# Expert rows of a decoder layer: gathered as quarters and turned in 32x32 blocks on VectorE instead of TensorE transposes

## The chip, the cores and the metric

The kernel is one program on one core of a Trainium2 chip. The core has a matrix engine (TensorE, "PE" in the profile, with its weight loads as "PEld"), VectorE ("DVE"), ScalarE ("ACT"), GpSimd ("POOL"), a queue engine ("SP") and 16 DMA engines that all queues share. The metric is the device time of one execution in microseconds (us); lower is better.

## The reference, cut to what matters

The program computes one layer of a hybrid decoder: a projection, differential attention, an S5 state-space branch, an output projection, and then a mixture of experts in which each of 2048 tokens goes to 2 of 32 experts. The change touches the last part alone:

```
order = jnp.argsort(flat_e)                       # assignments sorted by expert
rows = jnp.zeros((n_rows, 1024)).at[dest].set(h[stok])   # every expert padded to blocks of 128 rows
def expert_block(args):
    xb, e = args                                  # 128 rows of 1024 values, one expert
    hid = jax.nn.silu(xb @ w_gate[e]) * (xb @ w_up[e])   # w_gate, w_up: 1024 x 512
    return hid @ w_down[e]                        # w_down: 512 x 1024
out = segment_sum(expert_out * gate, stok)        # back to the tokens
```

Everything is fp32. A matmul is done as three matmuls in the faster fp32r format: each operand is split into a high part (rounded) and a low part (the rest), and hi x hi, hi x lo and lo x hi are summed.

## The kernel before, in words

The stages before the experts write the normalised tokens to a table in HBM, `h2`, of 1024 values a row. A routing stage (`route`) makes `ids`, a 128 x 64 tile in which column b holds the token of each of the 128 rows of block b, and `meta`, which holds for each block the ordinal of its expert. With the inputs timed here there are 49 blocks over 32 experts. `place(b)` is the ordinal of block b's expert; where it differs from the block before, the weights change. This text calls such a block a change of expert, and neighbouring blocks that each change the expert a run.

`experts` is written as one loop per engine. The engines meet in semaphores alone, and each engine carries out its instructions strictly in its written order. Iteration j of the loops handles the first two products of block j+1 and the last product of block j.

- TensorE, per iteration: `product(G, 0)` (24 matmuls of 512 columns with w_gate), `hidden_T(j)` (4 transposes of the hidden values), `product(U, 1)` (24 matmuls with w_up), `rows_T(0)` and `rows_T(1)` (8 transposes of 128x128 that turn the gathered rows `x` of the block after next into PSUM banks XT), `down(j)` (24 matmuls with w_down). A transpose of rows is needed since a matmul contracts over the partitions.
- ScalarE: `hidden_hi`, silu, `split_hi(0)` twice (the high part of w_gate, 128x2048 each, only on a change of expert), `rows_hi` twice (high part of the turned rows), `split_hi(1)` (w_up) around `out_half` (scaled output rows, waits for `down`), then `split_hi(2)` (w_down, an iteration after the change).
- VectorE: `hidden_lo`, `split_lo(0)` twice (low part of w_gate), `hidden` (silu times U, waits for U), `rows_lo` twice (low part of the rows, from PSUM), `split_lo(1)` twice, `split_lo(2)` twice.
- GpSimd: waits until the transposes have read `x`, then gathers the rows of the block after (`gather`: an index column is copied, then one indirect DMA of 128 rows of 4 KB); `add_rows` (waits for both `out_half`, then an indirect DMA adds 128 rows to `x1` in HBM), `gather_gate` (128 single values), and on a change of expert the two 1 MB loads of the next w_down, each after the `split_lo(2)` that frees its half.
- SP: the loads of the next w_gate and w_up, each half after the `split_lo` that frees it.

All buffers named here exist once: one `x`, one raw, one high and one low copy of each weight.

## Time and profile before

| | |
|---|---|
| Time, median of 3 runs | 2225.64 us (2224.3 to 2226.03) |
| Time of the profiled execution | 2227.88 us |
| Its span, first to last instruction | 2226.2 us |
| Expert stage within the span | about 1254.5 to 2154 us |
| Mean granted TensorE clock | 0.949 |
| TensorE busy | 2001.2 us, 90% |
| VectorE, ScalarE, GpSimd busy | 1416.8, 1073.5, 529.1 us |

The profiled execution took 2227.88 us, of which 1.68 us lie outside the span. The page's busy shares are averages over unlike stages, so the expert stage is read by itself.

### The profile page before, as it was taken

What the parts mean: (1) busy time and instruction counts of PE and PEld (TensorE: products, weight loads), DVE (VectorE), ACT (ScalarE), POOL (GpSimd) and SP (SyncE); (2) the same over time, 40 slices, a digit from 0 to 9 for tenths busy, and PEclk for the clock granted to TensorE, in tenths of its full rate; (3) what the DMA queues carried; (4) which work ended last, traced back from release to release, by engine and by line L of the source; (5) the groups of instructions that cost most, each with busy time, mean ns of one, the idle gap of its engine ahead of it and who ended that gap; (6) DMA issues with size and microseconds to landing.
All of it is one profiled execution on the core that took longest, in us unless ns stands there. A gap on an engine that the chain in (4) does not pass through costs nothing. (4 is left out here: it accounts for less than half of the span.)

```text
span 2226.2 us, 32053 instructions
## 1 busy us (share of the span) xinstructions
PE 2001.2 (90%) x10153; PEld 1677.8 (75%) x10154; DVE 1416.8 (64%) x2368; ACT 1073.5 (48%) x1591; POOL 529.1 (24%) x637
## 2 busy tenths in 40 slices
PE   6999999886798989869997599999999999999970
PEld 5888888785587878768886488888888888888860
DVE  4675687466697977946555766575668756445444
ACT  4332211234377777862322365565567655445443
POOL 2000111242000000000000244454445645334440
PEclk9999999998799999989998699999999999999995
DMA  8665986731464143024443597797879978576638
GB/s 251 221 223 203 304 299 228 244 150 29 130 154 109 48 101 77 1 79 138 142 153 151 179 363 252 267 337 270 289 255 389 343 270 314 178 248 223 230 81 315
DMA packets 170121, 458.37 MB, mean 206 GB/s; under 512 B 19872, under 2 KB 69104, under 8 KB 144432
## 3 DMA queue, kind: packets, MB, share of 16 engines
q1 hardware_dynamic: 122896, 285.30, 37.2%
q0 software_dynamic: 31008, 138.37, 20.2%
q10 hardware_dynamic: 16128, 33.56, 4.3%
q8 instruction: 50, 0.82, 0.1%
q14 instruction: 39, 0.32, 0.1%
HBM read 342.08 MB, written 115.10 MB: 205 GB/s over the span
## 5 line engine op out<-in xcount | busy, mean ns | idle before, releaser
L2208 DVE TENSOR_TENSOR w_down_lo<-w_down_raw,w_down_hi 128x2048 fp32r<-128x2048 f32 x64 | 144.1, 2288 | 122.9 <-ACT w_down_hi L2145 122.9
L1480 PE MATMUL c_bank<-v_head,map_T 128*128 128x128 f32 x1088 | 150.8, 282 | 24.1 <-ACT map_T L1390 21.3
L1480 PEld LDWEIGHTS c_bank<-v_head,map_T 128*128 128x128 f32 x1088 | 138.1, 194 | 39.3 <-ACT map_T L1390 32.0
L2208 DVE TENSOR_TENSOR w_gate_lo<-w_gate_raw,w_gate_hi 128x2048 fp32r<-128x2048 f32 x63 | 141.6, 2288 | 40.3 <-ACT w_gate_hi L2145 33.9
L2292 PE MATMUL m_bank<-w_down_hi,hidden_T_hi 128*128 128x512 f32 x392 | 160.4, 409 | 6.8 <-DVE w_down_lo L2208 6.8
L2271 PE MATMUL m_bank<-w_gate_hi,rows_T_hi 128*128 128x512 f32 x392 | 156.2, 399 | 6.4 <-DVE rows_T_lo L2213 3.9
L2271 PE MATMUL m_bank<-w_up_hi,rows_T_hi 128*128 128x512 f32 x392 | 158.8, 405 | 0.0
L2208 DVE TENSOR_TENSOR w_up_lo<-w_up_raw,w_up_hi 128x2048 fp32r<-128x2048 f32 x64 | 146.2, 2286 | 15.7 <-ACT w_up_hi L2145 15.7
L2272 PE MATMUL m_bank<-w_gate_lo,rows_T_hi 128*128 128x512 f32 x392 | 156.0, 398 | 0.0
L2273 PE MATMUL m_bank<-w_gate_hi,rows_T_lo 128*128 128x512 f32 x392 | 156.0, 398 | 0.0
L2293 PE MATMUL m_bank<-w_down_lo,hidden_T_hi 128*128 128x512 f32 x392 | 155.3, 396 | 0.0
L2273 PE MATMUL m_bank<-w_up_hi,rows_T_lo 128*128 128x512 f32 x392 | 154.8, 395 | 0.0
L2272 PE MATMUL m_bank<-w_up_lo,rows_T_hi 128*128 128x512 f32 x392 | 154.5, 394 | 0.0
L1450 PE MATMUL c_bank<-k_parts,q_parts 128*128 128x512 f32 (+3 forms) x320 | 132.2, 418 | 10.0 <-DMA k_parts<-kT_d 5.2
L1330 DVE CUSTOM_DVE_ANT_0 scores<-c_bank,alibi 128x512 f32<-128x512 f32 (+3 forms) x160 | 97.3, 608 | 46.2 <-PE c_bank L1451 40.3
L2160 ACT ACTIVATE rows_out<-m_bank,slot_gate 128x512 f32<-128x512 f32 x98 | 67.4, 688 | 106.0 <-PE m_bank L2297 106.0
L2145 ACT ACTIVATE w_up_hi<-w_up_raw 128x2048 fp32r<-128x2048 f32 x62 | 118.5, 1914 | 0.0
L1451 PE MATMUL c_bank<-k_parts,q_parts 128*128 128x512 f32 (+3 forms) x320 | 118.4, 376 | 0.0
L2145 ACT ACTIVATE w_down_hi<-w_down_raw 128x2048 fp32r<-128x2048 f32 x62 | 115.4, 1905 | 6.2 <-DMA w_down_raw<-in_w_down_dram 6.2
L2149 ACT ACTIVATE rows_T_hi<-m_bank 128x512 fp32r<-128x512 f32 x100 | 54.5, 596 | 129.7 <-PE m_bank L2264 129.6
L2145 ACT ACTIVATE w_gate_hi<-w_gate_raw 128x2048 fp32r<-128x2048 f32 x62 | 115.3, 1916 | 0.0
L2110 POOL DMA_INDIRECT x_d<-rows_out,to_idx x49 | 109.0, 2224 | 9.9 <-issue 9.9
(422 smaller groups left out, 5226.9 us busy)
## 6 DMA issues: line engine op xcount, KB each, us to landing
w_gate_raw<-in_w_gate_dram SPq DMA_DIRECT2D x64, 1024.0 KB, 7.0
w_down_raw<-in_w_down_dram POOLq DMA_DIRECT2D x64, 1024.0 KB
w_up_raw<-in_w_up_dram SPq DMA_DIRECT2D x64, 1024.0 KB, 8.1
hT_d<-hT_parts SPq DMA_DIRECT2D x32, 512.0 KB, 5.1
hT_parts<-hT_d SPq DMA_DIRECT2D x32, 512.0 KB, 9.2
k_parts<-kT_d SPq DMA_DIRECT2D x64, 256.0 KB, 8.2
u_tok<-in_x_dram SPq DMA_DIRECT2D x16, 512.0 KB, 5.3
qT_d<-qk_out ACTq DMA_DIRECT2D x32, 256.0 KB, 3.6
```

The source lines that it names most:

```text
L1330: dve.tensor_tensor_reduce(of(u, m, c * BANK, c * BANK + w), bank[2 * (n % 2) + m][:, 0:w], ramp[:, x0:x0 + w], SLOPES[h], -BIG, ALU.add, ...
L1450: pe.matmul(out, qt, k_of(4 * h + c, 0)[:, m, 0:w].bitcast(F32R), start=True, stop=False)
L1451: pe.matmul(out, qt, k_of(4 * h + c, 1)[:, m, 0:w].bitcast(F32R), start=False, stop=True).then_inc(qk_done, 1)
L1480: last = pe.matmul(out_of(u), aT[:, n % 2, b * P:(b + 1) * P], v[h % 2][:, kt], start=kt == 0, stop=kt == u % NT)
L2110: pool.indirect_dma_start(d["x1"], bass.IndirectOffsetOnAxis(ap=to_idx[:], axis=0), out[:], None, compute_op=ALU.add).then_inc(out_st, 16)
L2145: act.activation(whi[w][:, halves[i]], raw[w][:, halves[i]], ACT.Copy).then_inc(hi_done[w], 1)
L2208: dve.tensor_tensor(wlo[w][:, halves[i]], raw[w][:, halves[i]], whi[w][:, halves[i]], ALU.subtract).then_inc(lo_done[w], 1)
L2271: pe.matmul(to[:], xh[:, k], whi[w][:, c], start=k == 0, stop=False)
L2272: pe.matmul(to[:], xh[:, k], wlo[w][:, c], start=False, stop=False)
L2273: last = pe.matmul(to[:], xl[:, k], whi[w][:, c], start=False, stop=k == KT - 1)
L2292: pe.matmul(DN[h][:], hh[:, k], whi[2][:, part(k)], start=k == 0, stop=False)
L2293: pe.matmul(DN[h][:], hh[:, k], wlo[2][:, part(k)], start=False, stop=False)
```

## The change

From the third block on, a block's rows are no longer gathered as whole rows. `h2` is seen as a table of 4 x 2176 quarter rows of 256 values, and four indirect DMAs of 128 quarters (1 KB each) fill `x`: partition 32f + i gets, in its r-th quarter, the quarter f of row 32r + i. A 128x1024 tile that lies so needs only to be transposed inside 32x32 blocks, and VectorE does that in two instructions, `turn(0)` and `turn(1)`, 512 elements a partition each, from SBUF (stride of 8 elements) to a new SBUF tile `rows_T`. The 8 TensorE transposes leave the loop. `rows_hi` and `rows_lo` read `rows_T` in SBUF and no longer XT in PSUM. The indices of the quarters are made once, at the stage's start, in `part_rows` on VectorE, with 4 small matmuls on TensorE behind the first `product(G, 0)` and before the first `product(U, 1)`.

```diff
+    def gather_parts(self, pool, ones, part_ids, d, b):
+        pool.tensor_copy(self.part_idx[:], part_ids[:, bass.ds(b * PARTS, PARTS)]).then_inc(self.idx_set, 1)
+        pool.wait_ge(self.idx_set, b + 1)
+        pool.tensor_tensor(self.hold[:], ones[:, 0:1], ones[:, 1:2], ALU.add)
+        for r in range(PARTS):
+            pool.indirect_dma_start(self.x[:, r * PART:(r + 1) * PART], None, d["h2"].rearrange("r (f c) -> (r f) c", f=PARTS),
+                                    bass.IndirectOffsetOnAxis(ap=self.part_idx[:, r:r + 1], axis=0)).then_inc(self.x_in, 16)
...
 GpSimd, before the loop
-                for b in range(2):
-                    pool.wait_ge(xT_psum, 2 * b + 2)
-                    gather(b + 1)
+                pool.wait_ge(xT_psum, 2)
+                store.gather(pool, ones, ids, d, 1)
+                pool.wait_ge(part_set, 1)
+                pool.wait_ge(xT_psum, 4)
+                store.gather_parts(pool, ones, part_ids, d, 2)
 GpSimd, in the loop
-                    pool.wait_ge(xT_psum, 2 * j + 6)
-                    gather(j + 3)
+                    pool.wait_ge(turned, 2 * j + 2)
+                    store.gather_parts(pool, ones, part_ids, d, j + 3)
 ScalarE, in the loop
+                def rows_hi(h, want):
+                    act.wait_ge(turned, want)
+                    act.activation(xh[:, 4 * h:4 * h + 4], xT[:, 4 * h:4 * h + 4], ACT.Copy).then_inc(xh_done, 1)
...
-                    rows_hi(0, 2 * j + 5)
-                    rows_hi(1, 2 * j + 6)
+                    act.wait_ge(u_done, j + 2)
+                    rows_hi(0, 2 * j + 1)
+                    rows_hi(1, 2 * j + 2)
                     with where_below(nc, act, now, order):
-                        act.wait_ge(u_done, j + 2)
                         split_hi(1, order, 0)
 VectorE
+                def rows_lo(h, want):
+                    dve.wait_ge(xh_done, want)
+                    dve.tensor_tensor(xl[:, 4 * h:4 * h + 4], xT[:, 4 * h:4 * h + 4], xh[:, 4 * h:4 * h + 4],
+                                      ALU.subtract).then_inc(xl_done, 1)
+
+                def turn(h):
+                    dve.transpose(xT[:, 4 * h:4 * h + 4].rearrange("p k (r i) -> p r k i", r=PARTS),
+                                  x[:].rearrange("p (r j k) -> p r k j", r=PARTS, k=KT)[:, :, 4 * h:4 * h + 4]).then_inc(turned, 1)
+
+                def part_rows():
+                    dve.tensor_copy(pick[:], ident[:].rearrange("p (r o i) -> p r o i", r=PARTS, o=1).to_broadcast([P, PARTS, PARTS, QUAD])).then_inc(pick_set, 1)
...
+                    dve.wait_ge(part_psum, 1)
+                    dve.tensor_scalar(part_ids[:].rearrange("p (b r) -> p b r", r=PARTS), PI[:, 0:PARTS * NBLK].rearrange("p (r b) -> p b r", r=PARTS),
+                                      float(PARTS), quad[:, 0:1], ALU.mult, ALU.add).then_inc(part_set, 1)
...
                 split_lo(1, 0, 1)
+                part_rows()
                 split_lo(2, 0, 0)
 in the loop, after split_lo(0)
+                    dve.wait_ge(x_in, 64 * j + 96)
+                    dve.wait_ge(xl_done, 2 * j + 4)
+                    turn(0)
+                    turn(1)
                     hidden(j + 1)
 TensorE, after the first product(G, 0)
+                pe.wait_ge(pick_set, 2)
+                for r in range(PARTS):
+                    last = pe.matmul(PI[:, r * NBLK:(r + 1) * NBLK], pick[:, r].rearrange("p f i -> p (f i)"), ids_f[:], start=True, stop=True)
+                last.then_inc(part_psum, 1)
 TensorE, in the loop
-                    pe.wait_ge(x_in, 16 * j + 48)
-                    rows_T(0)
-                    rows_T(1)
                     down(j, before)
```

## Rows read from the trace of the kernel before

**Rows 1.** The page, part 1: busy time of each engine.
```profile
PE 2001.2 (90%) x10153; PEld 1677.8 (75%) x10154; DVE 1416.8 (64%) x2368; ACT 1073.5 (48%) x1591; POOL 529.1 (24%) x637
```

**Rows 2.** Windows: length, busy of PE, PEld, DVE, ACT, POOL, clock, DMA share, GB/s.
```profile
1254.50:2154.00 899.50, 889.17 (x4100) 728.39 (x4100) 551.08 (x387) 510.55 (x481) 428.00 (x498) 0.99 0.78 273
...
1701.00:1719.30 18.30, 18.30 (x86) 14.98 (x86) 15.57 (x10) 13.98 (x12) 10.57 (x12) 1.00 1.02 384
```

**Rows 3.** Groups of the loop, 1300 to 2190 us.
```profile
L2213 DVE TENSOR_TENSOR rows_T_lo<-m_bank,rows_T_hi 128x512 fp32r<-128x512 f32 x94 | 60.3, 683 | 6.9 <-ACT rows_T_hi L2149 6.9
...
L2264 PE MATMUL m_bank<-ident,rows_in 128*128 128x128 f32 x376 | 49.3, 274 | 0.0
...
L2045 POOL DMA_INDIRECT rows_in<-h_d,idx x46 | 46.2, 1005 | 11.3 <-issue 10.5
```

**Rows 4.** Timeline of PE over one iteration and the start of the next.
```profile
1610.52 0.63 PE L2281 MATMUL m_bank<-ident,hidden 128*128 128x128 f32 x4
...
1616.58 1.05 PE L2264 MATMUL m_bank<-ident,rows_in 128*128 128x128 f32 x8
1617.38 0.48 PE L2292 MATMUL m_bank<-w_down_hi,hidden_T_hi 128*128 128x512 f32 x1
1617.70 0.39 PE L2293 MATMUL m_bank<-w_down_lo,hidden_T_hi 128*128 128x512 f32 x1
...
1623.07 0.40 PE L2271 MATMUL m_bank<-w_gate_hi,rows_T_hi 128*128 128x512 f32 x1
...
1628.67 0.63 PE L2281 MATMUL m_bank<-ident,hidden 128*128 128x128 f32 x4
```

**Rows 5.** Timeline of DVE: a w_down split, then an iteration with a change of expert.
```profile
1335.34 4.49 DVE L2208 TENSOR_TENSOR w_down_lo<-w_down_raw,w_down_hi 128x2048 fp32r<-128x2048 f32 x2 [6.65 <-ACT w_down_hi L2145]
...
1630.90 0.69 DVE L2223 TENSOR_TENSOR hidden_T_lo<-m_bank,hidden_T_hi 128x512 fp32r<-128x512 f32 x1 [0.61 <-issue]
1632.26 4.50 DVE L2208 TENSOR_TENSOR w_gate_lo<-w_gate_raw,w_gate_hi 128x2048 fp32r<-128x2048 f32 x2 [0.68 <-ACT w_gate_hi L2145]
1636.67 0.68 DVE L2219 TENSOR_TENSOR hidden<-silu,m_bank 128x512 f32<-128x512 f32 x1
1637.27 1.28 DVE L2213 TENSOR_TENSOR rows_T_lo<-m_bank,rows_T_hi 128x512 fp32r<-128x512 f32 x2
```

**Rows 6.** Timeline of POOL: beside the w_down split above, and in a run.
```profile
1335.47 2.20 POOL L2099 COPY gate_idx<-slot_gate_ids 128x1 int32 x1
1337.76 2.13 POOL L2101 TENSOR_TENSOR hold<-ones 128x1 f32<-128x1 f32 x1
...
1685.21 1.03 POOL L2102 DMA_INDIRECT slot_gate<-gates_d,gate_idx  x1
...
1742.23 1.16 POOL L2080 DMA_DIRECT2D w_down_raw<-in_w_down_dram  x2
...
1757.30 3.05 POOL L2102 DMA_INDIRECT slot_gate<-gates_d,gate_idx  x1
```

**Rows 7.** Timeline of ACT: the second w_down half of the load at 1742.23.
```profile
1755.21 1.91 ACT L2145 ACTIVATE w_down_hi<-w_down_raw 128x2048 fp32r<-128x2048 f32 x1 [2.38 <-DMA w_down_raw<-in_w_down_dram]
```

**Rows 8.** Timelines of DVE and PE at the start of the expert stage.
```profile
1262.37 4.48 DVE L2208 TENSOR_TENSOR w_down_lo<-w_down_raw,w_down_hi 128x2048 fp32r<-128x2048 f32 x2
1271.47 4.50 DVE L2208 TENSOR_TENSOR w_gate_lo<-w_gate_raw,w_gate_hi 128x2048 fp32r<-128x2048 f32 x2 [4.62 <-ACT w_gate_hi L2145]
...
1230.58 1.01 PE L1913 MATMUL r_bank<-ident,block_facts 128*1 128x128 f32 x4 [4.17 <-DVE block_facts L1989]
...
1268.84 0.40 PE L2271 MATMUL m_bank<-w_up_hi,rows_T_hi 128*128 128x512 f32 x1
...
1278.07 0.47 PE L2271 MATMUL m_bank<-w_gate_hi,rows_T_hi 128*128 128x512 f32 x1 [2.57 <-issue]
```

**Rows 9.** PE after a long idle stretch, then windows beside it (columns as in rows 2).
```profile
711.64 1.22 PE L1480 MATMUL c_bank<-v_head,map_T 128*128 128x128 f32 x4 [3.40 <-ACT map_T L1390]
...
712.00:718.00 6.00, 6.00 (x26) 5.28 (x26) 5.36 (x10) 4.20 (x13) 0.00 (x0) 0.58 0.01 3
```

More of the change, by code:

```diff
@@ L43 @@
 NBLK = 64
+PARTS = 4
+PART = D // PARTS
+QUAD = P // PARTS
 MIN_BLK = 2 * SEQ // P
@@ L2049, in source, with experts @@
         return a[("w_gate", "w_up", "w_down")[w]][0, e].rearrange("o (p k) n -> p (o k n)", k=k)[:, self.halves[i]]
-def experts(nc, ident, ones, ids, gate_ids, meta, store, a, d):
+def experts(nc, ident, ones, const, ids, gate_ids, meta, store, a, d):
     with ExitStack() as ctx:
@@ L2056, in experts @@
         sem = ctx.enter_context(phase_semaphores(nc))
-        bank = [ctx.enter_context(nc.psum_tensor(f"m_bank{i}", [P, BANK], F32)) for i in range(7)]
-        G, U, XT, HT, DN = bank[0], bank[1], bank[2:4], bank[4], bank[5:7]
+        bank = [ctx.enter_context(nc.psum_tensor(f"m_bank{i}", [P, BANK], F32)) for i in range(8)]
+        G, U, XT, HT, DN, PI = bank[0], bank[1], bank[2:4], bank[4], bank[5:7], bank[7]
         FT = FF // P
@@ L2071, in experts @@
         g_done, u_done, d_done, silu_done, hid_done = (sem(n) for n in ("g_done", "u_done", "d_done", "silu_done", "hid_done"))
-        xT_psum, xh_done, xl_done, hT_psum = (sem(n) for n in ("rT_psum", "rT_hi_done", "rT_lo_done", "hidT_psum"))
+        xT_psum, turned, xh_done, xl_done, hT_psum = (sem(n) for n in ("rT_psum", "rows_turned", "rT_hi_done", "rT_lo_done", "hidT_psum"))
+        pick_set, part_psum, part_set = (sem(n) for n in ("row_of_quad_set", "part_ids_psum", "part_ids_set"))
         with nc.Block() as block:
@@ L2094, in _ @@
             def _(pool):
-                gather = lambda b: store.gather(pool, ones, ids, d, b)
                 def gather_gate(b, count):
@@ L2145, in split_hi, with first_rows_hi @@
                     act.activation(whi[w][:, halves[i]], raw[w][:, halves[i]], ACT.Copy).then_inc(hi_done[w], 1)
-                def rows_hi(h, want):
+                def first_rows_hi(h, want):
                     act.wait_ge(xT_psum, want)
                     act.activation(xh[:, 4 * h:4 * h + 4], XT[h][:].rearrange("p (k t) -> p k t", k=4), ACT.Copy).then_inc(xh_done, 1)
+                def rows_hi(h, want):
+                    act.wait_ge(turned, want)
+                    act.activation(xh[:, 4 * h:4 * h + 4], xT[:, 4 * h:4 * h + 4], ACT.Copy).then_inc(xh_done, 1)
                 def hidden_hi(want):
@@ L2162, in _ @@
                 act.preload_act_table(ACT.Silu)
-                rows_hi(0, 1)
-                rows_hi(1, 2)
+                first_rows_hi(0, 1)
+                first_rows_hi(1, 2)
                 first, second = place(act, 0), place(act, 1)
@@ L2170, in _ @@
                     split_hi(0, second, 1)
-                rows_hi(0, 3)
-                rows_hi(1, 4)
+                first_rows_hi(0, 3)
+                first_rows_hi(1, 4)
                 with where_below(nc, act, first, second):
@@ L2209, in split_lo, with first_rows_lo @@
                                       ALU.subtract).then_inc(lo_done[w], 1)
-                def rows_lo(h, want):
+                def first_rows_lo(h, want):
                     dve.wait_ge(xh_done, want)
@@ L2226, in _ @@
                 split_lo(1, 0, 0)
-                rows_lo(0, 1)
-                rows_lo(1, 2)
+                first_rows_lo(0, 1)
+                first_rows_lo(1, 2)
                 split_lo(1, 0, 1)
+                part_rows()
                 split_lo(2, 0, 0)
@@ L2236, in _ @@
                 hidden(0)
-                rows_lo(0, 3)
-                rows_lo(1, 4)
+                first_rows_lo(0, 3)
+                first_rows_lo(1, 4)
                 with where_below(nc, dve, first, second):
@@ L2440, in hybrid_layer @@
             route(nc, ident, ones, logits, const, ids, gate_ids, meta, store, a, d)
-            experts(nc, ident, ones, ids, gate_ids, meta, store, a, d)
+            experts(nc, ident, ones, const, ids, gate_ids, meta, store, a, d)
         finish(nc, a, d, out)
```

12 lines of the change are left out of this document (11 added, 1 removed).

## The prediction

> **What bounds the kernel now.** I read the page's busy times first: TensorE is busy for 2001.2 of 2226.2 us [rows 1]. Then the windows, since the change touches one stage: from 1254.5 to 2154 us TensorE is busy for 889.2 of 899.5 us at a granted clock of 0.99 (the 2.4 GHz level), DVE for 551, POOL for 428 [rows 2]. So TensorE sets this stage and what leaves its queue is worth its whole length, until another queue is late. Which one could be, I read from the timelines, each time counted from the start H of the four transposes of the hidden values. TensorE: H is 1610.52, the next H 1628.67: a period of 18.15 us, without a gap. The next product with w_gate starts at 1623.07, H + 12.55 [rows 4]. DVE in an iteration with a change of expert (H = 1628.67): the w_gate split starts at H + 3.59, `hidden` at H + 8.00, and `rows_lo` ends at 1638.55, H + 9.88 [rows 5]. The rows are ready 2.67 us ahead of the product that reads them. This slack is what the two turns are put into.
>
> In the DVE timeline 30 of the 48 iterations hold a w_gate split, and one more stands ahead of the loop. By iteration they are ahead, 0, 1; 3; 5; 7 to 10; 12; 14, 15; 17; 19 to 25; 27; 29 to 31; and every second one from 34 to 46, so there are two runs of three, one of four and one of seven. In the long run the DMA engines are at 1.02 of their time [rows 2], and a half of w_down whose load was issued at 1742.23 is first read at 1755.21, after ScalarE waited 2.38 us for it [rows 6, 7]. That is 13 us from issue to use; runs are near the DMA's limit already.
>
> **What is removed.** Eight transposes in each of 48 iterations (376 of these records stand in the window of [rows 3]). They run from 1616.58 to 1617.38, and the next matmul then takes 0.32 us to its follower where the pace of the stage is (1623.07 - 1617.70)/23 = 0.233. Without them the matmul at 1617.70 would start at 1616.58 + 0.23 = 1616.81: 0.88 us saved, 48 x 0.88 = 42.2 us, and a period of 17.27 [rows 4].
>
> **What is added to VectorE.** Two turns of 128x512. The trace holds no DVE transpose. The nearest row is `rows_lo`, the same size, 683 ns alone [rows 3], 1.28 for two [rows 5], so about 0.60 each in a row. I take 0.62, with 0.60 as the lower end (DVE moves the same number of elements) and twice that `rows_lo` pair's share, 1.28, as the upper (a read stride of 8 elements, a write in pieces of 32). With 0.62 each `rows_lo` ends at H + 9.88 + 1.24 = H + 11.1, and the product now wants it at 12.55 - 0.88 = H + 11.67. Outside runs the turns are covered, with 0.55 us left. An iteration without a split has the whole w_gate split (4.4 us) as cover.
>
> The Trainium skill (Vector Engine (DVE) Microarchitecture Reference, "3.8 The reshape front-end and per-opcode configuration") says that the transpose sustains one element a cycle and lane, which would put a turn beside `rows_lo` and leave the sum as it is; no row here shows it.
>
> `rows_hi` now waits for the turn, so ScalarE starts the w_up split near H + 9.9 and no longer at 7.7. U wants it at H + 17.3 + 6; covered. Moving its wait for U forward costs nothing, U ends at H + 6.1.
>
> **The start.** `part_rows` waits for four small matmuls behind the first `product(G, 0)`, which ends at 1268.8; four fp32 matmuls took 1.01 us in the routing [rows 8]. DVE gets on at about 1270.3. Behind it stand both w_down splits (4.48, before at 1262.37) and the w_gate split (4.4, before at 1271.47), then `hidden` and `rows_lo` (1.9): done at 1281.1 to 1281.5 where the next product started at 1278.07 [rows 8]. Price 3.5, once.
>
> **GpSimd.** A gather becomes four, each as many indices as one before: 1.0 us each [rows 3], so 3.0 us more an iteration. GpSimd is idle long enough by the sum (428 of 899.5 us busy), but its operations are held while a DVE split runs: beside the w_down split from 1335.34 to 1339.83 a one-column copy took 2.20 us and a one-column add 2.13, each to the end of a half [rows 5, 6], and an indirect DMA of 1.03 took 3.05 [rows 6]. The gathers are released by the turns at H + 9.3, and `rows_lo` (now two SBUF operands) and two w_up halves of 2.2 us follow at once. The first two get through by about H + 12.3, the third waits for the end of a half (14.2), the fourth for the next (16.5): finished at H + 17.5 where the one gather ended near H + 8.5. Outside runs DVE is then idle, the output add and the gate gather follow in 4 us, and the rows, wanted by `turn` and only by U's end before `hidden`, land in time. Covered.
>
> In a run they are not. Behind the gathers come `add_rows` and `gather_gate`, six operations held again by the w_down split and the next w_gate split (about 10 us), and behind these the w_down loads: issued at H + 28.6, that is the next H + 11, where now it is 4.6 (1742.23 against 1628.67 + 6 x 18.16 = 1737.6 [rows 4, 6]). The second half lands 11 to 13 us after (two halves of 2.5 us, each sharing the engines with SP's loads, and 1.3; or the 13 of [rows 6, 7]), at the next H + 22 to 24; ScalarE wants it at 16.7. Behind it on ScalarE are `hidden_hi`, silu and the next w_gate split, behind these DVE's split and the turns: `rows_lo` then ends at H + 16.9 and TensorE waits 5.2 us. I carried the five queues forward from iteration to iteration with these durations, 2.5 us of DMA time for a half of a weight (1 MB at 384 GB/s would be 2.7 [rows 2]) and 1.3 latency. The third block of a run costs 0.35, the iteration after it 2.4 where the run ends and 5.2 where it goes on; further ones alternate between 1.0 and 5.2, as each long wait lets GpSimd catch up. Two runs of three: 2 x 2.75 = 5.5. The run of four: 5.55. The run of seven: 0.35 + 5.2 + 1.0 + 5.2 + 1.0 + 2.4 = 15.15. Together 26.2.
>
> The Trainium skill (SBUF — State Buffer, "SBUF: two separate sides") calls the port pair that VectorE and GpSimd share an exclusive lock, taken by a VectorE operation with two SBUF inputs against a GpSimd operation that reads SBUF. The trace agrees, with the 2.20 and 2.13 us above. This is the rule that speaks against the change; without it the 26.2 would be 8 to 12 and the time 2197 to 2201, by it 2215.
>
> **The DMA.** Same bytes in four times the packets for the rows. The rows give no price for 1 KB packets; below I take none, above that they cost twice the time of 4 KB ones, which in the same carrying forward adds 1 us.
>
> **The clock.** After an idle stretch of 3.40 us the clock of 712 to 718 was 0.58 on average, near the 1.2 GHz level [rows 9]; after 2.57 us at 1278.07 it stayed up [rows 8]. The three 5.2 us waits split into a shorter one before the gate product and one before the next; I put 2 us on them, ends 0 and 8.
>
> **Sum,** against the profiled execution's own 2227.88 (span 2226.2 and 1.7 around it): -42.2 + 3.5 + 26.2 + 2.0 = -10.5, so 2217.4. The median of the runs is 2.2 below that execution: 2215.1.
>
> **Rivals.**
> - *The four gathers slip through.* If the held time is less than I carry (an indirect DMA needs the port only at moments, or the turns leave gaps), the w_down loads stay early and only DVE and the DMA engines limit runs, at about 18.3 a block. For it: 1.03 us is the common length of these operations. Against: the 3.05 [rows 6]. Runs then cost 8: -42.2 + 3.5 + 8 = -30.7, with DMA trouble of 4 to 5 in the run of seven about -26: 2200.
> - *Turns at twice the price* (the other side). At 1.28 each the rows are ready at H + 12.4, 0.77 late in each of 30 iterations, 23 us, and a run's chain is longer by 1.3, while the cover in the third blocks is used twice over (less 4): -10.5 + 23 - 4 = +8.5: 2234. From 1.1 us a turn on the kernel is slower than before. For it: a read stride of 8 elements and a new unit. Against: nothing but the like of `rows_lo`.
> - *The long runs collapse* further: w_down's late load collides with w_gate's and w_up's, which are wanted in the same 10 us, at DMA engines that are full. If every deep wait (8 iterations) grows by 2 us, +16: 2231.
> - *No change*: 2225, where a turn near 1.0 eats the gain (30 iterations at 0.2 and longer runs).
>
> **How the numbers follow.** The measurement tells about 0.2% (4.5 us) from no change. Sum as worked 0.47 (2207 to 2221); gathers slip through 0.15 (2198 to 2206); long runs collapse 0.12 (2221 to 2235); turns at twice or more 0.16 (2230 to 2250, more if four times); no change 0.10. Eight in ten is 2198 to 2238. Faster by over 0.2% (under 2221.2): 0.47 + 0.15 and a little of the others, 0.64; within: 0.14; slower: 0.22.
>
> **What would show it.** In the profile after: no L2264 transposes in the loop; periods of 17.27 where every second iteration changes the expert; a DVE transpose row near 0.6 to 0.7 us, 96 of them; four indirect DMAs an iteration, the later two over 2 us beside splits; PE idle before gate products only in runs, near 1468 and from 1690 to 1750, some 5 us, behind ScalarE waits for `w_down_raw`; the second gate product 3 us later. The prediction is wrong if the turns are longer than 0.9 us, if PE waits outside runs, or if the loads of w_down in runs are issued before H + 6.

## The result, and the profile after

The changed kernel is slower: 2262.43 us (median of 4 runs, 2259.16 to 2267.42) against 2224.97 (2223.7 to 2226.03); ratio 1.0171, 95% interval 1.0155 to 1.0187. 2215 was predicted, with 2198 to 2238 as the range of eight in ten. The profiled execution took 2261.87 us, its span is 2260.3, 34.1 more than before.

Busy times, from part 1 of the page of the changed kernel (beside [rows 1]), and its window of the expert stage, columns as in [rows 2]:

```profile
PE 1970.9 (87%) x9777; PEld 1640.3 (73%) x9778; DVE 1526.7 (68%) x2470; ACT 1076.6 (48%) x1591; POOL 802.6 (36%) x781
```

```profile
1254.50:2188.00 933.50, 859.18 (x3724) 691.77 (x3724) 661.59 (x489) 514.27 (x480) 700.32 (x642) 0.98 0.77 263
```

TensorE has 30 us less to do in the stage and the stage is 34 us longer: it now waits 74 us, and before 10. The groups of the stage say what grew:

```profile
L2056 POOL DMA_INDIRECT rows_in<-h_d,part_idx x192 | 287.4, 1497 | 55.5 <-issue 49.9 <-ACT rows_out L2179 4.0
...
L2241 DVE STREAM_TRANSPOSE rows_T<-rows_in 128x512 f32<-128x512 f32 x96 | 113.3, 1218 | 68.2 <-DMA rows_in<-h_d,part_idx 68.2
...
L2237 DVE TENSOR_TENSOR rows_T_lo<-rows_T,rows_T_hi 128x512 fp32r<-128x512 f32 x96 | 62.2, 691 | 0.1
```

A turn takes 1.218 us where `rows_lo` of the same size takes 0.69, and 0.683 before; a quarter gather takes 1.50 with 0.30 before it, where the one gather took 1.0 [rows 3]. The waits of the stage (total, times, longest) show three that the kernel before has not or hardly has:

```profile
DVE rows_T L2241 <- DMA rows_in<-h_d,part_idx: 68.2, 14, 6.9
...
ACT rows_out L2179 <- DMA slot_gate<-gates_d,gate_idx: 41.6, 31, 2.4
...
ACT w_down_hi L2160 <- DMA w_down_raw<-in_w_down_dram: 20.1, 16, 3.0
```

**Period by period.** I measure the loop from the first to the last start of the hidden transposes: 1283.76 to 2149.52 = 865.8 us before, 1288.09 to 2183.78 = 895.7 after. An iteration that waits for nothing takes 17.01 us (TensorE's timeline of the changed kernel, H, next product, next H):

```profile
1955.44 0.63 PE L2327 MATMUL m_bank<-ident,hidden 128*128 128x128 f32 x4
...
1966.98 0.39 PE L2317 MATMUL m_bank<-w_gate_hi,rows_T_hi 128*128 128x512 f32 x1
...
1972.46 0.63 PE L2327 MATMUL m_bank<-ident,hidden 128*128 128x128 f32 x4
```

With 47 such and the last of 11.54 the loop would be 811.0 us, 54.8 less than before; 84.7 are lost again. An iteration with a w_gate split outside runs loses 1.0 (H = 1937.40; DVE's timeline, then TensorE's):

```profile
1940.98 4.49 DVE L2227 TENSOR_TENSOR w_gate_lo<-w_gate_raw,w_gate_hi 128x2048 fp32r<-128x2048 f32 x2 [1.60 <-ACT w_gate_hi L2160]
1945.40 2.41 DVE L2241 STREAM_TRANSPOSE rows_T<-rows_in 128x512 f32<-128x512 f32 x2
1947.69 0.68 DVE L2260 TENSOR_TENSOR hidden<-silu,m_bank 128x512 f32<-128x512 f32 x1
1948.26 1.32 DVE L2237 TENSOR_TENSOR rows_T_lo<-rows_T,rows_T_hi 128x512 fp32r<-128x512 f32 x2
```

```profile
1949.88 0.47 PE L2317 MATMUL m_bank<-w_gate_hi,rows_T_hi 128*128 128x512 f32 x1 [0.78 <-issue]
```

The rows are ready at H + 12.2 and the product starts at H + 12.48, not at 11.54. In a run it is worse. In the iteration from H = 1679.30 (period 22.06, the next 23.94) GpSimd, ScalarE and TensorE show:

```profile
1681.08 1.59 POOL L2120 COPY to_idx<-slot_ids 128x1 int32 x1
1682.75 2.13 POOL L2122 TENSOR_TENSOR hold<-ones 128x1 f32<-128x1 f32 x1
1685.04 1.65 POOL L2123 DMA_INDIRECT x_d<-rows_out,to_idx  x1 [0.16 <-issue]
1686.11 1.62 POOL L2112 COPY gate_idx<-slot_gate_ids 128x1 int32 x1
1687.82 2.13 POOL L2114 TENSOR_TENSOR hold<-ones 128x1 f32<-128x1 f32 x1
1690.09 1.01 POOL L2115 DMA_INDIRECT slot_gate<-gates_d,gate_idx  x1
1691.10 1.20 POOL L2095 DMA_DIRECT2D w_down_raw<-in_w_down_dram  x2
```

```profile
1696.85 0.69 ACT L2179 ACTIVATE rows_out<-m_bank,slot_gate 128x512 f32<-128x512 f32 x1 [2.24 <-DMA slot_gate<-gates_d,gate_idx]
1697.43 1.90 ACT L2160 ACTIVATE w_up_hi<-w_up_raw 128x2048 fp32r<-128x2048 f32 x1
...
1700.86 1.92 ACT L2160 ACTIVATE w_down_hi<-w_down_raw 128x2048 fp32r<-128x2048 f32 x1 [0.94 <-DMA w_down_raw<-in_w_down_dram]
1705.77 1.92 ACT L2160 ACTIVATE w_down_hi<-w_down_raw 128x2048 fp32r<-128x2048 f32 x1 [3.00 <-DMA w_down_raw<-in_w_down_dram]
```

```profile
1710.25 0.50 PE L2338 MATMUL m_bank<-w_down_hi,hidden_T_hi 128*128 128x512 f32 x1 [2.74 <-DVE w_down_lo L2227]
```

`add_rows` and `gather_gate` stand behind the fourth gather and are held by VectorE's splits. The gate values are issued at H + 10.8 and used at H + 17.6, though the down product that they scale is done by then (ScalarE waits for the gate values, not for TensorE); behind that scaling on ScalarE stands the second half of the w_up split, behind it the w_down split, which then waits again, for the load issued at H + 11.8. GpSimd, held so often, is busy for 20.39 of the 22.06 us of this iteration.

### The profile page after: what moved, and what is told of

It reads as the page before. It is cut to its first block and busy times, and to the rows that moved or that the text cites. A ratio compares the mean times of both kernels' runs of the same rounds, so it can differ in the third digit from the quotient of the medians.

```text
span 2260.3 us, 31501 instructions
## 1 busy us (share of the span) xinstructions
PE 1970.9 (87%) x9777; PEld 1640.3 (73%) x9778; DVE 1526.7 (68%) x2470; ACT 1076.6 (48%) x1591; POOL 802.6 (36%) x781
## 5 line engine op out<-in xcount | busy, mean ns | idle before, releaser
L2056 POOL DMA_INDIRECT rows_in<-h_d,part_idx x192 | 287.4, 1497 | 55.5 <-issue 49.9
L2227 DVE TENSOR_TENSOR w_down_lo<-w_down_raw,w_down_hi 128x2048 fp32r<-128x2048 f32 x64 | 144.8, 2291 | 74.7 <-ACT w_down_hi L2160 51.6
L2168 ACT ACTIVATE rows_T_hi<-rows_T 128x512 fp32r<-128x512 f32 x96 | 60.5, 633 | 257.5 <-DVE rows_T L2241 218.5
L2241 DVE STREAM_TRANSPOSE rows_T<-rows_in 128x512 f32<-128x512 f32 x96 | 113.3, 1218 | 68.2 <-DMA rows_in<-h_d,part_idx 68.2
L1453 PE MATMUL c_bank<-k_parts,q_parts 128*128 128x512 f32 (+3 forms) x320 | 133.0, 420 | 10.8 <-DMA k_parts<-kT_d 6.6
L2317 PEld LDWEIGHTS m_bank<-w_gate_hi,rows_T_hi 128*128 128x128 f32 x392 | 76.1, 194 | 79.1 <-issue 64.0
```

The lines of the kernel that those rows point to most:

```text
L1453: pe.matmul(out, qt, k_of(4 * h + c, 0)[:, m, 0:w].bitcast(F32R), start=True, stop=False)
L2056: pool.indirect_dma_start(self.x[:, r * PART:(r + 1) * PART], None, d["h2"].rearrange("r (f c) -> (r f) c", f=PARTS), bass.IndirectOffsetO ...
L2227: dve.tensor_tensor(wlo[w][:, halves[i]], raw[w][:, halves[i]], whi[w][:, halves[i]], ALU.subtract).then_inc(lo_done[w], 1)
L2241: dve.transpose(xT[:, 4 * h:4 * h + 4].rearrange("p k (r i) -> p r k i", r=PARTS), x[:].rearrange("p (r j k) -> p r k j", r=PARTS, k=KT)[: ...
L2317: pe.matmul(to[:], xh[:, k], whi[w][:, c], start=k == 0, stop=False)
```

## The experiments

Sixteen kernels ran, each beside the kernel before. "Loop" is as above; the start of the loop differs between profiled executions by up to 15 us (1273 to 1288), so loops tell more than spans. The loop and the columns behind it are of one profiled execution each, the ratio is of the medians of all runs. The last three columns are what the periods have over the fastest one (17.01, or 17.78 in the four kernels from the pad on, 18.15 before): in 21 iterations with a w_gate split outside the deep part of runs; in 13 iterations of the deep part (the third block of a run and later, and the iteration behind it); in the 13 others without a split.

| kernel | ratio (95%) | loop | split | runs | others |
|---|---|---|---|---|---|
| before | | 865.8 | 0 | 0 | 0 |
| changed | 1.0171 (1.0155 to 1.0187) | 895.7 | 22.6 | 46.9 | 15.2 |
| no turn, one gather | 0.9943 (0.9925 to 0.996) | 849.0 | 1.8 | 36.2 | 0 |
| one gather | 1.0118 (1.0099 to 1.0137) | 884.5 | 24.9 | 48.6 | 0 |
| plain copies | 1.003 (1.0015 to 1.0045) | 872.3 | 3.1 | 50.2 | 8.0 |
| contiguous turns | 1.0072 (1.0048 to 1.0096) | 883.0 | 2.6 | 49.5 | 19.8 |
| start | 1.015 (1.013 to 1.0169) | 898.9 | 27.9 | 48.5 | 11.5 |
| no w_down loads | 1.0068 (1.0045 to 1.009) | 876.1 | 22.3 | 36.9 | 5.9 |
| one gate | 1.001 (0.9998 to 1.0022) | 865.7 | 23.5 | 30.2 | 1.0 |
| loads on SP | 1.0194 (1.0177 to 1.0212) | 906.6 | 45.7 | 45.3 | 4.6 |
| turn ahead | 1.0797 (1.0775 to 1.082) | 1042.8 | 35.0 | 96.3 | 94.7 |
| all three | 1.0533 (1.0514 to 1.0552) | 988.8 | 32.4 | 74.7 | 69.5 |
| before, pad | 0.9933 (0.9919 to 0.9947) | 848.0 | 0 | 0 | 0 |
| pad and four gathers | 1.005 (1.0031 to 1.0069) | 875.7 | 0 | 25.5 | 2.2 |
| pad and spare turns | 1.0087 (1.0067 to 1.0106) | 880.2 | 3.3 | 28.8 | 0 |
| pad and late release | 1.0032 (1.0017 to 1.0046) | 873.7 | 0 | 25.6 | 0.1 |

**No turn, one gather.**

```diff
-  pool.wait_ge(turned, 2 * j + 2)
+  pool.wait_ge(xl_done, 2 * j + 6)
-  turn(0); turn(1)
-  act.activation(xh[:, 4 * h:4 * h + 4], xT[:, 4 * h:4 * h + 4], ACT.Copy)   # rows_lo alike
+  act.activation(xh[:, 4 * h:4 * h + 4], x[:, BANK * h:BANK * (h + 1)]..., ACT.Copy)
```

> The changed kernel with one gather of whole rows a block and no turn: ScalarE and VectorE split the gathered rows as they lie (untransposed rows enter the products), the rest as in the changed kernel. What is left is what the removal of the transposes is worth. Theory: the shortest periods of the changed kernel, 17.01 us, are TensorE's own; with 47 of them and the last of 11.54, against 895.7 us now, and with the 33.4, 20.5 and 28 us of the other causes gone, the span is near 2260.3 - 82 = 2178 us, ratio to the kernel before 0.978. Rival: the prediction's 17.27 a period gives about 2190 (0.984); if the DMA engines alone hold the run of seven at 18.15 a block, 7 us more than either.

Measured 2211.39, above theory and rivals; the loop is 849.0, where 811 belongs to the theory's 2178. Outside runs every period but one (18.71) is 17.01, as the theory had it; the runs still lose 36. So neither turns nor four gathers are needed for that. Three differences from the kernel before are left in this one: the gather is released later (it waits for `rows_lo`, H + 9.9, and then meets the w_up split), the period is shorter, and `rows_lo` reads two SBUF operands. A later run takes the release alone. In the run of four ScalarE waits 4.7 us for the gate values:

```profile
1459.24 0.69 ACT L2177 ACTIVATE rows_out<-m_bank,slot_gate 128x512 f32<-128x512 f32 x1 [4.69 <-DMA slot_gate<-gates_d,gate_idx]
```

**One gather.**

```diff
-  for r in range(PARTS):
-      pool.indirect_dma_start(self.x[:, r * PART:(r + 1) * PART], ...)
+  pool.indirect_dma_start(self.x[:], None, d["h2"], ...)
```

> The changed kernel with its turns and its start, but one gather of whole rows a block in place of four of quarters (the turned rows are then not the reference's). Theory 'gathers': the turns alone cost 0.93 us in each of the 30 iterations that split w_gate, and the late rows and the late w_down loads come from the four gathers; so 54 us go away: span near 2206, ratio 0.991, faster than the kernel before. Rival 'turns': the turns make the runs and the second iterations late by themselves, since they release the gather later (H + 10.4 instead of 8.6); then the span stays over 2235 (ratio over 1.004).

Measured 2249.18. The rival is right on runs (48.6) and the theory on the others (0): with one gather the rows land in time, and the other columns stay about as they were. The 15 us of the "others" are the four gathers'.

**Plain copies.**

```diff
-  dve.transpose(xT[:, 4 * h:4 * h + 4].rearrange(...), x[:].rearrange(...)...)
+  dve.tensor_copy(xT[:, 4 * h:4 * h + 4], x[:, BANK * h:BANK * (h + 1)]...)
```

> The changed kernel with its four gathers, each turn replaced by a plain copy of the same 128x512 (rows not turned). The only copy of this size in the trace took 0.41 us, so the pair should take 0.8 and not 2.40. Theory 'gathers': only the 28 us on VectorE's chain go away and a little in runs, span 2225 to 2232, ratio 1.000 to 1.003. Rival 'turns': 2190 to 2205, ratio 0.984 to 0.991.

Measured 2231.74, within the theory's range; its ten runs lie between 2223.87 and 2237.07. The copies take 425 ns, the split iterations lose 3 us and no longer 23, the runs as much as before.

**Four gathers in the kernel before.**

```diff
-  gather(j + 3)
+  store.gather_parts(pool, ones, part_ids, d, j + 3)   # indices 4 * id + r: same rows, same places
```

> The kernel before, with its TensorE transposes, but each block's rows gathered by four indirect DMAs of quarter rows from the third block on (each partition still holds its own row, the result is unchanged); four small VectorE operations make the indices. Theory 'gathers': GpSimd's chain is 4 to 8 us longer, the w_down loads of runs come late although nothing is turned: 2236 to 2250, ratio 1.005 to 1.011. Rival: with the slack of the old order (period 18.15, rows wanted 24 us after the release) the four gathers are hidden and the time is the kernel before's, 2224 to 2228.

Measured 2236.78, in the theory's range, but the profile had something else: TensorE's period was 17.78 with all of its transposes in it. In both kernels it has no gap outside runs; the matmuls follow each other faster. The new tiles had moved those behind them in SBUF. That called for a run of its own.

**The kernel before with a pad.**

```diff
+  pad = sb("pad", [P, 8])
   xh, xl = sb("rows_T_hi", ...), sb("rows_T_lo", ...)
```

> The kernel before with one unused tile of 32 bytes a partition ahead of the tiles of the split rows, and nothing else. In the kernel before, the four tiles that TensorE loads as stationary operands (split rows and split hidden values) begin 32 bytes past a multiple of 64 in their partition and its matmuls of 512 columns follow each other at 0.2333 us; in the kernel with four gathers and transposes they begin at multiples of 128 and follow at 0.2275. Theory 'address': the pace comes from where these tiles begin, so the period falls from 18.15 to 17.78 without any change to the work, 48 x 0.37 = 17.8 us: span near 2208, ratio 0.992. Rival: the pace comes from something else of that kernel (its gathers' traffic, its timing), and this one stays within 2 us of the kernel before.

Measured 2210.46 (2207.42 to 2211.38), 14 us faster than the kernel before, with the same instructions. In a window of 35 us TensorE starts 168 matmuls where it started 164 before (window row of the padded kernel; columns: busy, clock, DMA, GB/s):

```profile
1925.00:1960.00 35.00, 35.00 (x168) 1.00 0.70 236
```

It beats both kernels of the case. It also gives the four gathers their own price: 875.7 - 848.0 = 27.7 us, nearly all in runs.

**w_down loads on SP's queue.**

```diff
+  sp.wait_ge(lo_done[2], 2 * o - 1 + i)      # behind the w_gate and w_up loads of o + 1
+  sp.dma_start(raw[2][:, halves[i]], ...)
-  pool.wait_ge(lo_done[2], 2 * now + 1 + i); load(pool, 2, e, i)
```

> The changed kernel with the w_down loads issued from SP's queue (behind the w_gate and w_up loads of the expert after) and no longer from GpSimd's behind the gathers. Theory 'queue': late w_down loads and rows that wait in GpSimd's DMA queue behind 2 MB of w_down are most of the 54 us that four gathers and runs cost; 28 us of the turns stay, and a few us in the long run for the DMA engines: span 2208 to 2220, ratio 0.992 to 0.997. Rival: the runs are held by the gate values that come late behind add_rows, and by the held gathers themselves; then under 25 us go away, span over 2235.

Measured 2268.05, on the rival's side. The early loads did what they should: nothing waits for a w_down load any more. But the gate values come later than ever, the runs lose 45.3 as before, and the split iterations outside them 45.7 where they lost 22.6 (waits, then DMA issues of SP and GpSimd, then ScalarE's timeline):

```profile
ACT rows_out L2179 <- DMA slot_gate<-gates_d,gate_idx: 97.9, 28, 7.3
```

```profile
1328.91 2.53 SPq L2116 DMA_DIRECT2D w_down_raw<-in_w_down_dram  x2
```

```profile
1333.09 1.01 POOL L2125 DMA_INDIRECT slot_gate<-gates_d,gate_idx  x1 [0.15 <-issue]
```

```profile
1341.75 1.26 ACT L2179 ACTIVATE rows_out<-m_bank,slot_gate 128x512 f32<-128x512 f32 x2 [7.29 <-DMA slot_gate<-gates_d,gate_idx]
```

The gather of 128 numbers is issued at 1333.09, 4 us behind a load, and its numbers are used 8.66 us later; the w_down split of ScalarE and behind it VectorE's stand behind that. So the loss in runs does not need a late w_down load. That late gate values alone are enough for it is not shown, since GpSimd's operations are held here too.

**Turns one iteration ahead.**

```diff
-  turn(0); turn(1)          # ahead of hidden(j + 1)
   hidden(j + 1); rows_lo(0, 2 * j + 5); rows_lo(1, 2 * j + 6)
+  dve.wait_ge(x_in, 64 * j + 160); dve.wait_ge(xl_done, 2 * j + 6)
+  turn(0); turn(1)          # rows of block j + 3
```

> The changed kernel with the turns of a block moved one iteration ahead, to the place behind rows_lo and before the w_up split, where VectorE waits 1 to 2 us for ScalarE in iterations outside runs; the gathers are released by them at about H + 12.3 of the iteration before and may take a whole period. One more gather at the end keeps the counts. Theory: the turns leave the chain in front of the w_gate product, 28 us go away, and the rows land before they are turned, another 20; in runs the w_up split is up to 1.5 us later: span 2212 to 2225, ratio 0.994 to 1.000. Rival: the held gathers and the late w_down loads move with the release and the runs cost more than now; span over 2235.

Measured 2402.75, on the rival's side and far beyond it, and not in runs alone. With one buffer for the rows, the gather is released by a turn and wanted by the next, one period on, and now the w_up split stands behind that wait (VectorE, then GpSimd of this kernel):

```profile
1946.08 2.08 DVE L2243 STREAM_TRANSPOSE rows_T<-rows_in 128x512 f32<-128x512 f32 x2 [7.24 <-DMA rows_in<-h_d,part_idx]
```

```profile
1967.75 8.85 POOL L2122 TENSOR_TENSOR hold<-ones 128x1 f32<-128x1 f32 x1
```

TensorE meets the late low part of w_up in the product U of the iteration behind, and this is nearly all that it waits for:

```profile
PE m_bank L2323 <- DVE w_up_lo L2229: 171.6, 28, 12.5
```

VectorE's wait for the rows costs 15.2 us where `hidden` stands behind it, in the iterations without a split of the changed kernel, and far more where a weight split does.

**All three.** The two edits before, the last operation of `part_rows` behind the w_down split, and a pad of 64 bytes.

> The two edits before together, the result of part_rows taken behind the w_down split (so that VectorE doesn't wait 5.5 us for the small matmuls), and an unused tile of 64 bytes so that the split hidden values begin at a multiple of 128 bytes. Theory: every period is 16.9 to 17.0 us outside the long run, which the DMA engines hold near 18; no late start: 2164 to 2180 us, ratio 0.973 to 0.980. Rival: GpSimd's chain, held by the splits, still sets the runs; 2195 to 2210.

Measured 2344.23, above the rival's range too: 58 us less than with the turns ahead alone and worse than all else. Which of the other three edits gave the 58 is not separated. The 64 bytes did not make the down products faster either, though `hidden_T_hi` then begins at a multiple of 128 bytes.

**Contiguous turns.**

```diff
-  dve.transpose(xT[...].rearrange("p k (r i) -> p r k i", ...), x[:].rearrange("p (r j k) -> p r k j", ...)[:, :, 4 * h:4 * h + 4])
+  dve.transpose(xT[:, 4 * h:4 * h + 4].rearrange("p k t -> p (k t)"), x[:, BANK * h:BANK * (h + 1)])
```

> The changed kernel with both turns reading and writing 512 elements in one piece (no stride of 8, no pieces of 32); the rows are then not turned rightly. A turn takes 1.218 us in the changed kernel and a plain copy of 128x512 takes 0.41. Theory 'unit': the transposing itself is the price, so a turn stays at 1.15 to 1.22 and the time within 3 us of the changed kernel's. Rival 'stride': it falls to 0.6 or less, and the time to that of the kernel with plain copies, 2228 to 2236.

```profile
L2241 DVE STREAM_TRANSPOSE rows_T<-rows_in 128x512 f32<-128x512 f32 x96 | 62.3, 687 | 55.3 <-DMA rows_in<-h_d,part_idx 55.1 <-issue 0.2
```

The rival is nearly right on the turn: 0.687 us, as long as `rows_lo` (0.682 here) and 0.26 more than a plain copy; the other 0.53 us of the changed kernel's turn come from the access pattern. The time, 2243.37, is above the rival's range: split iterations are as cheap as with copies (2.6), but the others lost 19.8 in the profiled execution, one of the longer ones (2245.61; the six lie between 2232.42 and 2245.79). So even turns as cheap as the prediction took them leave this kernel 0.7% slower than the one before.

**Spare turns in the padded kernel.**

```diff
+  turn(0); turn(1)          # spare_T <- spare_in, TensorE's transposes stay
   hidden(j + 1)
```

> The kernel before with the 32-byte pad (span 2209.8, period 17.78), with two turns of an unused tile put into each iteration of VectorE's loop, where the changed kernel has its turns; TensorE still transposes and one gather is released by it. VectorE's work in an iteration of a run is then 15.7 + 2.4 = 18.1 us against a period of 17.78. Theory 'VectorE is full': outside runs the rows are ready at H + 12.3, just at the product, and nothing is lost; in runs each iteration is 0.3 to 2 us longer and the w_down loads come later: 2218 to 2232. Rival: the turns alone are covered as the slack of 2.45 us says: within 3 us of 2210.

Measured 2244.75, 34 us over the padded kernel and above the theory's range. Outside runs they are nearly covered (3.3), in the 13 deep iterations they cost 28.8. VectorE and GpSimd, in the run of four:

```profile
1441.18 4.53 DVE L2210 TENSOR_TENSOR w_up_lo<-w_up_raw,w_up_hi 128x2048 fp32r<-128x2048 f32 x2
1445.58 4.53 DVE L2210 TENSOR_TENSOR w_down_lo<-w_down_raw,w_down_hi 128x2048 fp32r<-128x2048 f32 x2
```

```profile
1442.61 7.55 POOL L2109 COPY to_idx<-slot_ids 128x1 int32 x1 [3.85 <-ACT rows_out L2162]
```

With the turns, VectorE's four splits follow each other without a gap, and a one-column copy is held through all of them.

**Late release in the padded kernel.**

```diff
-  pool.wait_ge(xT_psum, 2 * j + 6)
+  pool.wait_ge(xl_done, 2 * j + 6)
```

> The kernel before with the pad and one change: the gather waits for rows_lo of VectorE (H + 9.9) and no longer for TensorE's transposes (H + 6.9), so that its two small operations and its DMA meet the w_up split. Theory 'release': this alone makes GpSimd's chain late in runs (gate values and w_down loads near the next H + 9 and not H + 3), and seven iterations of runs take 21 to 23 us as in the kernel with no turn and one gather: 2232 to 2245. Rival: with the period of 17.78 and not 17.01 GpSimd catches up, within 4 us of 2210.

Measured 2229.17, 19 us over the padded kernel in the medians, 25.7 in the loop (this execution's loop began 10 us early, which its span shows). The release alone is enough for a loss of this size, as the theory said; the median is 3 us below its range.

**The start.**

```diff
   part_rows()               # without its last wait and operation
   split_lo(2, 0, 0); split_lo(2, 0, 1)
+  part_rows_end()
```

> The changed kernel with the last operation of part_rows behind the w_down split and no longer ahead of it, so that VectorE doesn't wait 5.5 us for the small matmuls. Theory: the first loop iteration starts 4.3 us earlier (1283.8 where it is 1288.1) and nothing else changes: 2256 to 2259. Rival: it is made up for in the first run of three iterations, and the end stays within 1 us of the changed kernel's.

Measured 2256.88 us, within the theory's range, but the 5.5 us to the changed kernel are not clear of noise (1.0130 to 1.0169 against 1.0155 to 1.0187), and "nothing else changes" does not hold: in the profiled execution the loop begins 7.3 us earlier (1280.79) and is 3.2 us longer.

**No w_down loads, and one gate.** Then it was open what holds the runs.

```diff
-  pool.wait_ge(lo_done[2], ...); load(pool, 2, e, i)      # no w_down loads
```

> The changed kernel without the loads of w_down in the loop: w_down of the first expert is split again for each later one, so the down products of later experts are of the wrong weights. Theory 'w_down late': the long iterations of runs (23.9 to 25.7 us) fall to 18 to 19, as ScalarE no longer waits for the load; with less DMA traffic the rows land earlier outside runs as well: loop 50 us shorter, time 2208 to 2222. Rival 'VectorE full or gate late': the long iterations stay over 20 us and the time over 2235.

```diff
-  gather_gate(j + 1, j + 2)                               # one gate
```

> The changed kernel with the gate values gathered once: the loop gathers none, so all later blocks are scaled by the gate values of the first, and GpSimd has three operations fewer in an iteration. Theory 'w_down late' (the loads come 3 to 6 us earlier, as GpSimd's chain ahead of them is shorter by what gather_gate takes): 2225 to 2240. Rival: the gate values are not what holds, and with the four gathers held as before the time stays over 2255.

Measured 2238.75 and 2226.46. Without a single w_down load the runs still lose 36.9 of 46.9 and long periods are up to 22.5, as the rival had it: "w_down late" is not the main cause. Without the gate gather they lose 30.2, the others 1.0 and not 15.2, and the kernel is level with the one before. That run takes away the wait of ScalarE and three operations of GpSimd at once, and brings the w_down loads forward (in the iteration at 1679.30 from H + 11.8 to H + 5.7); it does not say which of these gave how much.

These runs also say something of the rows outside runs. The w_down loads stand just ahead of the row gathers in GpSimd's queue, and where they are gone from there or are issued earlier, the others lose less than the 15.2 of the changed kernel: 4.6 (loads on SP), 5.9 (no loads), 1.0 (one gate).

**Other pads.** `pad` of 40 and of 72 columns in the kernel before.

> The kernel before with an unused tile of 160 bytes a partition in place of 32: the split rows begin at an odd multiple of 128 bytes in their partition. Theory '128': the pace is that of the 32-byte pad, 0.2275 a matmul, 2208 to 2213. Rival '256 or more': 0.233 as in the kernel before, 2222 to 2227.

> As the run before, with 288 bytes: the split rows begin at an odd multiple of 256 bytes. Theory '256 is enough': 2208 to 2213. Rival '512 or 1024 is needed' (the quick ones began at multiples of 1024): 2222 to 2227.

Measured 2222.84 (2219.01 to 2228.16; ratio 0.9993, 0.9981 to 1.0006) and 2208.48 (2205.99 to 2212.9; 0.9925, 0.9899 to 0.995). The window with 160 and with 288 bytes:

```profile
1925.00:1960.00 35.00, 35.00 (x164) 1.00 0.69 235
```

```profile
1925.00:1960.00 35.00, 35.00 (x168) 1.00 0.70 236
```

With 160 bytes the pace stays slow, with 288 it is fast. The traces show no addresses; where a tile begins is worked out from the program's layout, by the sizes of the tiles ahead of it. What the runs alone show is that 32 bytes and 288 bytes of shift help and 160 do not.

## Why the prediction was wrong, step by step

- **The bound of before** was right. That a queue other than TensorE's would take over was said, too; how soon, was not.
- **What is removed: right, with a second gain that was not seen.** In the padded kernel (fast pace, with transposes) they still take 0.89 us: 1965.50 to 1966.31, and 0.31 for the next matmul where the pace is 0.23; 0.88 was predicted.

```profile
1965.50 1.05 PE L2265 MATMUL m_bank<-ident,rows_in 128*128 128x128 f32 x8
1966.31 0.48 PE L2293 MATMUL m_bank<-w_down_hi,hidden_T_hi 128*128 128x512 f32 x1
1966.62 0.40 PE L2294 MATMUL m_bank<-w_down_lo,hidden_T_hi 128*128 128x512 f32 x1
```

  The period fell by 1.14, not 0.88: the new tiles also moved `rows_T_hi` and `rows_T_lo`, by the program's layout to multiples of 256 bytes, and 48 of the 72 matmuls of 512 columns follow at 0.228 and not 0.233 us. That is 0.25 a period, 12 us. That is luck; by this sum the change would have cost about 50 us without it.
- **The turns: the size failed.** 1.22 us and not 0.62. The rival "turns at twice the price" had the price right, the stride of 8 as its reason, and its 0.77 late in each split iteration is 0.94 here; its time, 2234, was too low, since it took the runs as in the sum. The break-even at 1.1 us a turn is wrong: with contiguous turns of 0.687 the kernel is still 0.7% slower than the one before, with copies of 0.425 it is 0.3%. A contiguous turn takes as long as `rows_lo`, so the nearest row was the right one for the transposing and the wrong one for the pattern. The Trainium skill's one element a cycle and lane (Vector Engine (DVE) Microarchitecture Reference, "3.8 The reshape front-end and per-opcode configuration") fits the contiguous turn, which takes as long as `rows_lo` over as many elements (0.687 and 0.682), and not the strided one (1.218). The Trainium skill (SBUF — State Buffer, "Door 1: The DMA port swizzle") also says that SBUF is read in lines of 16 bytes and that each access to a new line pays: here each element read is 32 bytes from the last. The trace agrees in direction (1.218 against 0.687); the write in pieces of 32 changed with it and was not tried alone. This rule should have been weighed.
- **The start: right,** 4.3 us (1288.09 - 1283.76) for 3.5 predicted (its own times, 1281.1 to 1281.5 against 1278.07, give 3.0 to 3.4).
- **"Outside runs the rows land in time. Covered": failed.** The gathers whose rows were waited for ended mostly at H + 18.3 to 20.6, not 17.5, and the rows were used mostly about 6 us after the last of them was issued. No row gives the 1.3 us of latency that the prediction added to a transfer. VectorE waited 68.2 us for rows, and the 13 iterations without a split lose 15.2 us. With one gather they lose nothing. The prediction had the w_down loads late in runs alone; outside them, too, they are mostly issued at H + 9.3, some 2 us ahead of the gathers of these rows and by the same engine. That the 15.2 fall to 1.0 to 5.9 in the three runs with those loads away or earlier speaks for them as a part of the cause; what SP's loads, which run at the same time, add is not separated.
- **The runs: the step "behind the gathers come `add_rows` and `gather_gate`" failed, in who waits for them.** The issue of the w_down loads came about as predicted (H + 28.6, the next H + 11): in the 13 deep iterations the first half is issued seven times at H + 9.3 to 11.8, and six times at 5.0 to 6.8, three of them before the H + 6 that was named as a sign against the prediction. But the only waiting work that was carried forward was the w_down split. The gate values are wanted by `out_half(0)`, on ScalarE ahead of the second half of the w_up split, and they came late 31 times, 41.6 us of ScalarE's waiting in all; in the kernel before not once. 46.9 us were lost in the deep part of runs where 26.2 were predicted. Three single edits of the padded kernel each cost nearly this predicted sum by themselves: the later release 25.6, four gathers 25.5, turns on VectorE 28.8. In all three the w_down loads in iterations 9, 21 and 31 of the loop, each the third of a run, are issued at H + 9.3, where the padded kernel has them at 3.3: GpSimd's chain meets VectorE's splits. In the kernel before the gather passed between the w_gate split, which ends at 1636.76 [rows 5], and the w_up split from 1638.47 (GpSimd, then VectorE, same iteration):

```profile
1637.24 1.03 POOL L2045 DMA_INDIRECT rows_in<-h_d,idx  x1 [0.17 <-issue]
```

```profile
1638.47 2.28 DVE L2208 TENSOR_TENSOR w_up_lo<-w_up_raw,w_up_hi 128x2048 fp32r<-128x2048 f32 x1
```

- **The DMA: "four times the packets" did not come.** Between 1300 and 2150 us the changed kernel has 41442 packets and the kernel before 39874, and none between 512 B and 2 KB, so the quarters of 1 KB do not move as packets of their own:

```profile
DMA packets 41442, 228.13 MB, mean 268 GB/s; under 512 B 7824, under 2 KB 7824, under 8 KB 19376
```

- **The clock: the size failed.** In the loop 40 matmuls of 512 columns follow at 0.42 us on average in place of 0.23: 7.7 us, where 2 was taken. They are five stretches, all in the deep part of runs, behind waits of TensorE of 2.4 to 3.4 us; behind three others, of 2.1 to 2.5 us, the clock stayed up. One such stretch (columns: busy, clock, DMA, GB/s), with the granted clock at its lower level:

```profile
1711.60:1714.90 3.30, 3.30 (x10) 0.50 0.96 381
```

- **The sum.** Predicted: -42.2 + 3.5 + 26.2 + 2.0 = -10.5. Measured: -54.8 (42.7 for transposes, 12 for the pace), + 4.3 start, + 22.6 for the turns in split iterations, + 15.2 for late rows, + 46.9 in runs (the clock's 7.7 is within these): +34.2, and the spans differ by 34.1. Against the prediction the turns give 22.6 more, the late rows 15.2, the runs with the clock 18.7, the start 0.8 more, and what is removed, by the pace, 12.6 less. Its run of four is summed without the iteration behind the run, which the other runs have at 2.4; that one lost nothing. The signs of the rivals were seen one by one (turns +8.5, long runs collapse +6); that both could happen together, since both act on the same chain, was not: the range ended at 2238.

What stays open: how the 46.9 us of runs divide. With w_down loads never late (loads on SP) 45.3 are lost, with none at all 36.9, without the gate gather 30.2: the loads alone are the smaller part, and the gate values, GpSimd's chain and VectorE's work (18.82 us busy in the iteration from 1679.30, against a period of 17.01) share the rest in a way that no run here separates. Two row buffers, or gate values gathered a block ahead, were not tried.

## What to carry to other kernels

A step that is moved from one engine to another changes who releases the work behind it. Ask of each released operation what it will collide with there, and follow every reader of every operation that gets later, not the last load alone. Slack is spent once: later release, more gathers and added VectorE work all stand on the same gap of GpSimd's between two VectorE splits; each alone costs 25 to 29 us in runs, and the changed kernel with all three 46.9. And before a gain or a loss of 1% is put down to an edit, look at the pace of the untouched matmuls, since new tiles move old ones.

## What the runs showed of the hardware that was not expected

- Matmuls of 512 columns, whose stationary operand (fp32r, 128x128) is loaded anew for each, follow at 0.227 to 0.229 us on average where its tile begins, by the program's layout, at a multiple of 256 bytes in the partition, and at 0.232 to 0.234 where it begins at other multiples of 32, 64 or 128. Within the changed kernel the products that read `rows_T_hi` and `rows_T_lo` have the first pace and the down product the second. 32 unused bytes made this kernel 0.67% faster, 288 bytes 0.75%, and 160 nothing.
- VectorE turns 128x512 fp32 in 32x32 blocks in 0.687 us where both sides are contiguous, and in 1.218 us with a read stride of 32 bytes and a write in pieces of 32 elements. A plain copy takes 0.425.
- A VectorE split holds GpSimd's operations, and now and then several splits do. In the loop of the kernel before 76 of 282 copies and adds of one column took over 1 us and none over 2.4; two of them, 2.20 and 2.13 us, each end with a half of a split [rows 5, 6]. With the spare turns 14 took over 3 us, the longest 8.97, with the turns ahead 3 and with all three edits 6, and in no other kernel any: a copy was held 7.55 us and an add 8.85, each through four halves in a row. A missing gap between the halves is not enough for this, since there is none in [rows 5] either; what decides is open. The Trainium skill (SBUF — State Buffer, "SBUF: two separate sides") calls it an exclusive lock which whoever starts first gets for the whole instruction. The waits for a single half agree; that the waiting side can be passed over several times the rule does not say.
- Indirect DMAs issued one behind the other on GpSimd stand 0.30 us apart, besides 0.95 to 1.0 us each when nothing holds them: four cost 4.8 us and not 4.
